# Expert results back to token rows: one-hot products on chip in place of scatters to DRAM

## The reference

```
_, g_idx = lax.top_k(group_logits, 1)               # one of 4 groups
top_vals, top_idx = lax.top_k(within, TOP_K)        # two of its 8 experts
combine = sum(one_hot(expert_ids, 32) * w_top)
for e in range(N_EXPERTS):
    hid = silu(ht @ e_gate[e]) * (ht @ e_up[e])     # 1024 -> 512
    out = out + combine[:, e:e+1] * (hid @ e_down[e])   # 512 -> 1024
x = x + gt2 * out;  y = rmsnorm(x, final_norm_g)
```

## Time and profile before

| | |
|---|---|
| median of 3 runs | 1506.15 us (1504.37 to 1506.59) |
| span of the profiled execution | 1501.2 us; its own whole time is not listed apart, the three timed runs lie 3.2 to 5.4 above this span |
| TensorE busy | 1338.2 us (89%), mean granted clock 0.951 |
| VectorE, ScalarE, GpSimd busy | 587.7, 456.8, 233.8 us |
| DMA | 323.05 MB, of it 289.53 MB on SyncE's and ScalarE's hardware queue q1 |

### The profile page before, as it was taken

The page is one execution under the profiler, slowest core; times in us unless marked ns, Lnnn a source line. Parts: engine busy times, 40 slices in busy tenths (PEclk is TensorE's granted clock), DMA queues, the critical chain, the costliest instruction groups (busy, mean ns, idle before and its releaser), DMA issues. The chain is left out here.

```text
span 1501.2 us, 30378 instructions
## 1 busy us (share of the span) xinstructions
PE 1338.2 (89%) x13419; PEld 988.7 (66%) x13419; DVE 587.7 (39%) x1040; ACT 456.8 (30%) x730; POOL 233.8 (16%) x248
## 2 busy tenths in 40 slices
PE   5899999999999997888779999879888887888877
PEld 2778999999998997777769997743333333333332
DVE  3322134552235455556545667523222121121215
ACT  2334245555654553433344542200000000000002
POOL 3000000000112124234211102001111111111104
PEclk9999999999999998999999999869999998999989
DMA  8556452234422210000412481399999999999995
GB/s 311 190 186 222 153 179 83 71 109 126 133 86 71 71 36 19 4 4 4 135 44 72 142 249 53 151 402 425 426 427 427 426 427 427 427 428 425 428 402 206
DMA packets 128634, 323.05 MB, mean 215 GB/s; under 512 B 13865, under 2 KB 99075, under 8 KB 112594
## 3 DMA queue, kind: packets, MB, share of 16 engines
q1 hardware_dynamic: 114304, 289.53, 50.3%
q10 hardware_dynamic: 7522, 15.57, 3.0%
q0 software_dynamic: 6672, 15.95, 2.9%
HBM read 303.51 MB, written 25.11 MB: 219 GB/s over the span
## 5 line engine op out<-in xcount | busy, mean ns | idle before, releaser
L848 PE MATMUL bank<-upper2end 128*128 128x272 f32 x3168 | 419.8, 292 | 5.4 <-DVE upper2end L1089 5.4
L848 PEld LDWEIGHTS bank<-upper2end 128*128 128x128 f32 x3168 | 403.9, 190 | 27.5 <-issue 26.2
L2706 PE MATMUL bank<-upper7b,lower 128*64 128x512 f32 x912 | 255.9, 658 | 72.3 <-issue 71.5
L2706 PEld LDWEIGHTS bank<-upper7b,lower 128*64 128x64 f32 x912 | 84.3, 151 | 207.2 <-issue 205.4
L1066 DVE TENSOR_TENSOR upper2end<-upper,upper2end 128x1024 fp32r<-128x1024 f32 x66 | 81.7, 1238 | 286.0 <-ACT upper2end L612 285.9
L2514 ACT ACTIVATE lower<-bank 128x256 f32<-128x256 f32 x32 | 12.3, 383 | 437.8 <-PE bank L2715 437.8
L3073 DVE COPY lower<-bank 128x512 f32<-128x512 f32 x32 | 22.1, 691 | 277.2 <-PE bank L2706 277.2
L2569 PE MATMUL bank<-upper_r 128*128 128x272 f32 x768 | 103.1, 294 | 3.2 <-DVE upper_r L2968 3.2
L2569 PEld LDWEIGHTS bank<-upper_r 128*128 128x128 f32 x768 | 99.4, 191 | 5.9 <-DVE upper_r L2800 3.6
L2728 PE MATMUL bank<-upper7b,lower 128*64 128x512 f32 x432 | 98.3, 596 | 0.0
L2325 POOL DMA_INDIRECT expert_out<-lower x30 | 44.4, 1481 | 219.9 <-DVE lower L3096 210.0
(11 more groups left out here) (417 smaller groups left out, 1778.1 us busy)
## 6 DMA issues: line engine op xcount, KB each, us to landing
upper7b<-in_expert_w_gate SPq DMA_DIRECT2D x29, 2048.0 KB, 31.0
upper7b<-in_expert_w_up SPq DMA_DIRECT2D x28, 2048.0 KB, 32.8
upper7b<-in_expert_w_down SPq DMA_DIRECT2D x27, 2048.0 KB, 27.8
upper<-in_w_in SPq DMA_DIRECT2D x66, 512.0 KB, 3.7
lower<-in_w_ada SPq DMA_DIRECT2D x23, 1024.0 KB, 4.8
lower<-in_expert_w_down SPq DMA_DIRECT2D x5, 2048.0 KB, 30.2
lower<-in_expert_w_up SPq DMA_DIRECT2D x4, 2048.0 KB, 36.6
lower<-in_expert_w_gate SPq DMA_DIRECT2D x3, 2048.0 KB, 30.8
```

The lines of the kernel that those rows point to most:

```text
L848: m = mm(psum[s][:, c, 0:HALF], w_part[s][:, k, :], h_part[:, k, c * HALF:(c + 1) * HALF], start=k == 0 and w_part is w_high and h_part is ...
L2706: m = nc.tensor.matmul(psum[s][64 * b:64 * b + 64, 1, :], x_t[(e // 2) % 2][:, k, s * BLK:(s + 1) * BLK], w[:, k, :], start=k == 0, stop=k ...
```

## The change

Scatters, the table, its zeroing, the read-back and the sums over it go. Instead:

- **Codes.** Each row gets for each of its two experts the number 1024 x (expert + 1) + place in the expert. Twenty small TensorE instructions (ten fp32 products with the identity, after the routing) spread these numbers over all partitions, ScalarE copies them to `code_rows`. GpSimd makes `tgt`, the number that each of the 64 slots of each expert looks for.
- **One-hots** (`one_hots`, VectorE, four operations of 128x640 for each pair): comparing the codes with `tgt` gives 0/1 matrices `oh_t` of slots by rows.
- **Parts.** ScalarE copies y to a rounded fp32r part, VectorE subtracts it from y for the rest (`y_parts`), for the experts 0 to 29.
- **Products** (`rows_added`, TensorE). For each of the first 15 pairs and each of the 5 row tiles there are 8 fp32r matmuls (two experts, two parts, two column halves) into the two banks of `psum[3]`, 64 contraction rows and 128 result rows each; an fp32r matmul is one instruction. VectorE adds each tile to the residual (`rows_summed`, 128x1024) before the next tile's products may start. They are placed inside the `gate_up` of the odd experts from 3 on, for the pair before the running one.
- The hidden transposes and the down product use one bank pair (`psum[2]`) for all experts, since `psum[3]` is taken. Unit 6 has another place and waits for the last logits and the stored rows.

The diff, cut:

```
@@ sync
+                sp.wait_ge(lg_mm, 5)
+                sp.wait_ge(h2_kept[0], 48)
+                sp.wait_ge(h2_kept[1], 32)
                 load_unit(sp, 6)
-                sp.wait_ge(idx_done, 3)
+                sp.wait_ge(idx_done, 2)
+                sp.wait_ge(rt_const, RT_TARGETS)
                 load_unit(sp, 7)
...
-                    for s in range(2):
-                        sp.wait_ge(y_out9[s], r * (16 * Y_USES[s]) + 16 * Y_USES[s])
-                        sp.sem_inc(held, 1)
-                    for j, n in TILES:
-                        sp.dma_start(gath[j][0:n].rearrange("t k d -> t (k d)"), ys_v[j * P:j * P + n]
-                                     ).then_inc(gathered[j], 16)
@@ gpsimd
-                    refill(r, 1)
-                    for e in range(E_LAST):
-                        if e % 2 == 0 and e // 2 + 2 < NP:
-                            refill(r, e // 2 + 2)
-                        scatter(r, e)
-                    for j, n in TILES:
-                        g = gath[j]
-                        pool.wait_ge(gathered[j], r * 16 + 16)
-                        pool.sem_inc(held, 1)
-                        pool.tensor_tensor(g[0:n, 0, :], g[0:n, 0, :], g[0:n, 1, :], ALU.add).then_inc(g_sum, 1)
+                    for p in range(1, NP):
+                        refill(r, p)
@@ scalar
+                act.wait_ge(code_mm, 1)
+                for k in range(2):
+                    nc.scalar.activation(code_rows[k][:, 0:4, :].rearrange("p i t -> p (i t)"), bank(6 + k), ACT.Copy
+                                         ).then_inc(code_out, 1)
...
                         if 1 <= e < NE - 1:
                             coef_of_prompt(r, e + 1)
+                        if e < E_LAST:
+                            act.wait_ge(y_done, r * NE + (e + 1))
+                            nc.scalar.activation(y_parts[s][0], y_full, ACT.Copy).then_inc(yh_done, 1)
@@ tensor
+                for k in range(2):
+                    for i in range(5):
+                        row = bank(6 + k)[:, i * P:(i + 1) * P] if i < 4 else bank(4)[:, k * P:(k + 1) * P]
+                        m = mm(row, code[:, k, i:i + 1].broadcast_to([P, P]), ident, start=True, stop=True)
+                m.then_inc(code_mm, 1)
...
+                PRODUCTS_AT = [1, 3, 5, 7]
+
+                def rows_added(r, pair, j):
+                    n = 5 * pair + j
+                    if j == 0:
+                        pe.wait_ge(yrest_done, r * E_LAST + (2 * pair + 2))
+                        pe.wait_ge(oh_done, r * NE + (2 * pair + 2))
+                    if n:
+                        pe.wait_ge(moe_added, r * ADDS + n)
+                    for h in range(2):
+                        for part in range(2):
+                            for b in range(2):
+                                half = slice(BLK * b, BLK * b + BLK)
+                                m = nc.tensor.matmul(psum[3][:, b, :], oh_t[half, h, AT[j], :],
+                                                     y_parts[h][part][half, :], start=h + part == 0,
+                                                     stop=h + part == 2)
+                    m.then_inc(moe_mm, 1)
+
                 def gate_up(r, e):
                     s = e % 2
+                    pair = e // 2 - 1 if s and e >= 3 else None
+                    if e == NE - 1:
+                        for j in range(5):
+                            rows_added(r, pair, j)
...
                     for k in range(KD):
+                        if pair is not None and e < NE - 1 and k in PRODUCTS_AT:
+                            rows_added(r, pair, PRODUCTS_AT.index(k))
...
                     m.then_inc(gu_mm, 1)
+                    if pair is not None and e < NE - 1:
+                        rows_added(r, pair, 4)
...
                     last_down(r, 1, 0, False)
-                    gathered_sum(r, 1, False)
                     last_down(r, 0, 1, True).then_inc(last_mm, 1)
                     last_down(r, 1, 1, True).then_inc(last_mm, 1)
@@ vector
+                    ve.tensor_tensor(y_of(e), psum[2][:, 1, :], coef[s], ALU.mult).then_inc(y_done, 1)
+                    if e < E_LAST:
+                        v.wait_ge(yh_done, r * E_LAST + (e + 1))
+                        ve.tensor_tensor(y_parts[s][1], y_full, y_parts[s][0].bitcast(F32), ALU.subtract
+                                         ).then_inc(yrest_done, 1)
+
+                def one_hots(r, pair):
+                    if pair:
+                        v.wait_ge(moe_mm, r * ADDS + 5 * pair)
...
+                    for e in (2 * pair, 2 * pair + 1):
+                        ve.tensor_scalar(oh_t[:, e % 2], code_rows[0], tgt[:, e:e + 1], None, ALU.is_equal
+                                         ).then_inc(oh_half, 1)
+                    for e in (2 * pair, 2 * pair + 1):
+                        v.wait_ge(oh_half, r * NE + (e + 1))
+                        ve.scalar_tensor_tensor(out=oh_t[:, e % 2], in0=code_rows[1], scalar=tgt[:, e:e + 1],
+                                                in1=oh_t[:, e % 2].bitcast(F32), op0=ALU.is_equal, op1=ALU.add
+                                                ).then_inc(oh_done, 1)
+
+                def rows_summed(r, pair, j):
+                    n = TILES[j][1]
+                    v.wait_ge(moe_mm, r * ADDS + (5 * pair + j + 1))
+                    ve.tensor_tensor(x2[0:n, j, :], x2[0:n, j, :], psum[3][0:n].rearrange("t b c -> t (b c)"), ALU.add
+                                     ).then_inc(moe_added, 1)
...
+                        if e % 2:
+                            if e < NE - 1:
+                                one_hots(r, e // 2)
+                                gate_up_copied(r, e + 1)
+                        else:
+                            before = 5 if e + 2 == NE else 4
+                            if e:
+                                for j in range(before):
+                                    rows_summed(r, e // 2 - 1, j)
                             gate_up_copied(r, e + 1)
+                            if e:
+                                for j in range(before, 5):
+                                    rows_summed(r, e // 2 - 1, j)
+                            if e + 2 < NE:
+                                rows_copied(r, e // 2 + 1)
+                            else:
+                                one_hots(r, e // 2)
```

More of the change, by code:

```diff
@@ L1853, in build @@
         m_high, m_rest = y_high[0], y_rest[0]
-        lay_out_upper("7b")
+        gt1_b = Region(LOWER).take(2, D)
+        shift2_b = Region(LOWER + 2 * D).take(2, D)
+        NE, NGR, EPG, FF = 32, 4, 8, 512
+        tmp = Region(LOWER + 4 * D + 256, LOWER + MID - 4 * D)
+        g8 = tmp.take(5, 8)
+        top_g = tmp.take(5, 8)
+        top_e = tmp.take(5, 8)
+        pexp = tmp.take(5, 4)
+        psum_g = tmp.take(5)
+        both = tmp.take(5, NE)
+        cmax = tmp.take(1)
+        ROW_WORDS = 2 * 5 * P + 4 * 512
+        lay_out_upper("7b", ROW_WORDS)
         y_r = p_rw[:, 0:8]
@@ L1918, in build @@
         x2 = Region(x2_at, LOWER).take(5, D)
-        late = Region(base + 24 * TP - 512, x2_at)
-        router = late.take(KD, 36)
-        slot_rhs = [late.take(5, 2, NE) for _ in range(2)]
-        gt1_b = Region(LOWER).take(2, D)
-        shift2_b = Region(LOWER + 2 * D + 128).take(2, D)
+        router = Region(base + 24 * TP - 512, x2_at).take(KD, 36)
+        rhs_at = x2_at - 2 * 5 * NE
+        late = Region(rhs_at, x2_at)
+        slot_rhs = [late.take(5, NE) for _ in range(2)]
         scale2_b = Region(base).take(2, D)
@@ L1938, in build @@
         x_idx = route.take(NP)
-        y_idx = route.take(NE)
+        code = route.take(2, 5)
         slot_w = route.take(2, NE)
@@ L1952, in build @@
         slot_iota = small.take(P)
-        yb = small.take(1)
         eps_col = small.take(1)
@@ L1957, in build @@
         half_mean = small.take(5)
-        rows = [small.take(5, 2) for _ in range(2)]
+        rows = [small.take(5) for _ in range(2)]
+        tgt = small.take(NE)
         valid = small.take(5)
@@ L2016, in weights_of @@
             return Region(unit_at(kind, e)).take(*((4, D) if kind == "down" else (KD, FF)))
-        G_AT = [unit_at("down", NE - 4), unit_at("gate", NE - 2), unit_at("up", NE - 2), unit_at("down", NE - 3)]
-        gath = [Region(G_AT[j // 2] + (j % 2) * 2 * D).take(2, D) for j in range(5)]
-        fin_g = Region(G_AT[2] + 2 * D).take(D)
-        x_fin = [Region(G_AT[3] + j * D).take(D) for j in range(4)] + [Region(G_AT[2] + 3 * D).take(D)]
+        x_fin_at, fin_g_at = unit_at("down", NE - 3), unit_at("up", NE - 2) + 2 * D
+        fin_g = Region(fin_g_at).take(D)
+        x_fin = [Region(x_fin_at + j * D).take(D) for j in range(4)] + [Region(fin_g_at + D).take(D)]
         fin_junk = Region(unit_at("gate", NE - 1)).take(D)
@@ L2113, in next_slots @@
             v.wait_ge(pos_oh_done, 2 * r + 2)
+            if first(r):
+                v.wait_ge(code_done, 1)
```

(17 more changed lines are left out.)

201 lines of the change are left out of this document (63 added, 138 removed).

## The result

The changed kernel took 1512.99 us (median of 4 runs, 1509.26 to 1514.8), the one before 1505.26 in the same session (4 runs, 1504.03 to 1506.59): ratio 1.0052, 95% interval 1.0037 to 1.0068, so it is slower by 0.4 to 0.7%. The same kernel, run again beside a later experiment, gave 1.0056 (1.0041 to 1.0072). The profiled execution lasted 1509.26 us, the fastest of its four, with a span of 1507.5, 6.3 over the span of before. The medians are 7.7 apart; in every run that lists both, the whole time is 1.7 to 1.9 over the span, so the profiled execution of before took about 1503 and is a fast one too.

What follows compares the result with a forecast made beforehand. The weight stream was taken to bound the expert stage at 31.3 us a pair; afterwards TensorE's 30.6 and the stream's 30.65 nearly tie. Down product +9.5, tail -3.1: +6.4 us on the span, 1512 us, range 1499 less 1 to 1526.

Steps and rivals of the forecast that it cites:

- the bare groups: Last pair's five product groups ahead of the last gate_up, not hidden under other work: 12.7 us in all.
- the start: Beginning of the expert stage, up to gate_up(3) at 1029.7: no change taken, about 0.8 us later or 2 us earlier possible.
- The period: TensorE's time for each pair of experts: 23.5 + 6.1 products + 1.0 waits = 30.6 us.
- The forecast of a group: Eight fp32r matmuls on two row halves: 0.94 us, plus shape changes of 0.2 behind and 0.1 ahead, 1.24 us.
- The stream: Weight stream's time for each pair of experts: 30.65 us without scatters, against 31.3 before.
- the term for the scatters: What removing scatters gives the weight stream: 0.65 us a pair, 9.8 us by the last unit; at most 1.3 a pair.
- The second rival: More waits than seen, or a lower clock, in bare groups and gate_up: +4 to +11 us, 1516 to 1523; chance 0.22.
- The main case: TensorE's pair 30.6 us against the stream's 30.65, five bare groups at the end: 1512 us; chance 0.41.
- The tail: From the last down product to the end: 3.1 us shorter, without the identity product and with a shorter VectorE run.
- Cheap products: Rival: a group costs 0.86 + 0.2 us, TensorE's pair 29.7, ending at 1503 or 1499 us; chance 0.27.
- Row halves that don't overlap: Rival: fp32r row halves run one after the other, a group takes 2.17 us, the whole 1582 us; chance 0.06.
- Weight loads not hidden: Rival: each pair of product matmuls takes one load more, 0.76 us a group, the whole 1569 us; chance 0.04.

Runs made afterwards that it cites:

- the regrouped products: Changed kernel with three product groups inside each odd gate_up, one behind it and one after the next row transposes: 1495.9 us, ratio 0.9934 to the kernel before.
- The filler run: Kernel before with twenty filler instructions (ten fp32 products with the identity) where TensorE waits for the first gather: 1506.77 us, ratio 0.9998.
- the filled run: Changed kernel with fp32 filler products of 512 and 128 columns ahead of each of the last five product groups: 1509.12 us, ratio 1.0017 to the kernel before.
- the last two runs: Changed kernel with the row halves' products one after the other, 1513.67 us; and with all eight products of a group on one row half, 1585.3 us.
- the run that forbids the overlap: Changed kernel with all eight products of a group on the lower 64 contraction rows: 1585.3 us, ratio 1.0555 to the kernel before.

## Why the prediction came out as it did

The time (1513 for 1512) was right, and so was the mechanism: TensorE's pair and the stream's came out nearly equal, and the bare groups at the end decide. That the sum fits so closely is luck. Two sizes behind it were wrong and cancelled: the start came 4.4 us earlier than assumed, the bare groups took 3.5 longer. The period added 1.1.

- **The period** was to be 30.6 and is 30.68. The forecast of a group was 0.94 + 0.2 behind + 0.1 ahead = 1.24. Measured: 1.13 to the next row, and ahead of it 0.15 (an odd `gate_up` in pieces takes 1.08 + 3 x 1.87 + 1.08 = 7.77 instead of 7.02, shared by five groups), 1.28. For a pair that is 6.4 us of products, forecast 6.1: the changes of shape ahead of the groups were undersized, 0.75 for 0.4. The waits were to be 0.6 + 0.4 and are 0.49 + 0.31. 23.5 + 6.4 + 0.8 = 30.7, the 30.68 of the chain.
- **The stream** was to need 30.65 without scatters and needs 30.36: the term for the scatters was 0.65, measured 1.0 by the chain and 0.8 by the weight queue (the kernel before without them). It changed nothing here, since TensorE leads, but it decides what a better placement can win: where the regrouped products need 29.88 a pair, the stream is the limit late in the stage, as the waits there show. DMA share was to fall to 1.0 or below and is 1.01: the stream can run 0.3 us a pair faster than TensorE, and fifteen pairs of that only shorten the queue of units in flight, without emptying it.
- **The start** was taken at nothing, and is 4.4 us earlier: `gate_up(3)` starts at 1025.28, forecast 1029.7. The clock is up behind the code products, which I had as the lower bound of 2 us. The filler run shows that part, 2.35. The rest, about 2, is there before TensorE's first new instruction (986.59, the row ahead of it 1.96 us earlier than before), and most of it is no effect of the change: the 36 matmuls of the output projection start 1.3 us earlier in this execution (940.52 for 941.84), and in the executions of the other variants of the changed kernel, with the same work up to there, between 939.83 and 945.60. The gain from these matmuls to `gate_up(1)` is 1.9 to 3.3 us in all of them. So part of the 4.4 is the chance of one execution, and so is the fit of +6.3 to +6.4 us on the span; the medians differ by 7.7.
- **The bare groups** were to take 12.7 us and take 16.2. Their waits are 1.50 and four of 1.32, 6.8 in all, under the 7.8 expected; the groups fill 9.4 instead of 4.9. Of these 4.5 us some 3.4 are the clock, which falls to 1.2 GHz between the waits; the other 1.1 are the ends of the groups, which I had counted in the waits. The second rival named this drop at 2 us in the groups and 1.7 in `gate_up`; it is 3.4 (16.2 against the filled run's 12.8) and 0.8. The main case had priced five groups at full clock in a stretch where TensorE works 4.7 of 12.7 us: that term failed.
- So TensorE is ready for the last `gate_up` at 1454.8 instead of 1458.1, and starts it at 1470.96, forecast 1470.8.
- **The tail** was to be 3.1 us shorter and is 3.7: last down product's end to the end of the span 23.35 before (1477.85 to 1501.2), 19.7 after. Sum: the last down product ends 10.0 us later, the tail is 3.7 shorter, +6.3; forecast +9.5 - 3.1 = +6.4.
- **The rivals.** Cheap products did not come, as a group with its changes is 1.28, over the 1.15 that decides. Row halves that don't overlap: refuted by the last two runs; their price was forecast at 1582, and the run that forbids the overlap took 1585. Weight loads not hidden: in that run eight loads in a row go into one row half, and the group is still 2.04 us, which is eight lengths of 0.234 and 0.17 for the change, with no room for a load. The Trainium skill ("TensorE: Matmul & The Clock Gate", Part 3, The mechanism) says that a load overlaps running matmuls only where the row group differs; in that run all eight are in the same row half, and the loads are hidden all the same.

Where the gain of the scatters went is thus shown. Without products the new kernel takes 1489 us. The products give back 24, and the traces place 22.8 of them. From `gate_up(1)` until TensorE is ready for the last `gate_up` the changed kernel needs 453.0 us; without products that run starts after 444.1. Of these 8.9 us 4.4 arise in the first pair with products, while weights still lie ready, and then 0.35 a pair on average. The bare stretch adds 16.2, in which no weights are awaited. The last `gate_up` is 2.3 shorter (7.8 for 10.06). Placing the same products under other work returns 17 of the 24.

## What to carry to other kernels

When a change moves work from DMA to an engine with slack, compare the two periods after the move, not the slack before; here they came out within 0.3 us of each other, and where the work was placed decided the sign. The same products cost 1513 us in one order and 1496 in another: put each group where the engine has other work during the wait that follows it, above all at the end of the program, where nothing catches up. A stretch of short work and waits costs twice, by the waits and by the lower clock; price its work at both levels.

## What was not expected of the hardware

- Filling TensorE's waits with needless products made the program 0.4% faster, by the clock (0.50 without, 1.00 with them, from 1465 to 1470 us of either).
- The two halves of the contraction rows work side by side even when four products of one half are issued ahead of the four of the other (1.14 us against 2.04 on one half). The Trainium skill ("TensorE: Matmul & The Clock Gate", Part 3, The mechanism) has matmuls start and end strictly in the order of issue. 1.14 us leaves no room for that: the second four could then start only after three of the first, 0.70 us in, and need 0.86 to 0.94 more, 1.6 in all; and the trace has two matmuls under way from the group's first tenth of a us on. This takes it that the instructions reach TensorE in the program's order; over more than four instructions nothing was tried.
- Scatters that hold 2.6% of the DMA engines' time in the middle of the stage cost the weight queue 2.5% of its bytes there, and no more; the share of the earlier trace rows, a mean over a longer window, had it lower.
